# A second, root-scaled copy of the FFN input with its high and low halves side by side, and 512-column products from up piece 6 on

## What is computed

```python
h = rms_norm(x, ffn_pre_norm[l])
u = h @ w_up                                   # 1024 -> 5632
u = sum(up[:, t:t + S] * conv_w[t] for t in range(3))   # along the tokens
gate, val = jnp.split(u, 2, axis=-1)
x = x + rms_norm((jax.nn.gelu(gate) * val) @ w_down, ffn_post_norm[l])
```

## Time and profile before

| | us |
|---|---|
| median of 3 runs | 1029.5 (1029.44 to 1029.59) |
| span of the profiled execution | 1027.2 |
| TensorE busy in the span | 1013.0 (99%) |
| VectorE busy | 680.7 (66%) |
| ScalarE busy | 587.5 (57%) |
| GpSimd busy | 130.7 (13%) |
| moved from HBM | 168.7 MB |

### The profile page before, as it was taken

How to read it: one execution, slowest core, us unless ns; L and a number is a source line. 1 busy time by engine, 2 the same in 40 slices (tenths; PEclk the granted TensorE clock), 3 DMA queues, 4 the chain that set the end, 5 groups by cost and what they waited for, 6 DMA issues and landing times.

```text
span 1027.2 us, 15935 instructions
## 1 busy us (share of the span) xinstructions
PE 1013.0 (99%) x6244; PEld 908.5 (88%) x6244; DVE 680.7 (66%) x932; ACT 587.5 (57%) x859; POOL 130.7 (13%) x257
## 2 busy tenths in 40 slices
PE   8999999999999999999999999999999999999997
PEld 7889999888888999999888899998888889999996
DVE  5635566655596887878865355666555869787877
ACT  5657666565446654555575666565653457455553
POOL 3353124000002000000025221230000020000000
PEclk9999999999999999999999999999999999999999
DMA  8554345444444646555454534464344645545551
GB/s 259 178 177 155 122 141 168 161 165 164 144 150 157 203 169 203 170 200 172 168 190 159 174 124 128 150 205 164 124 144 164 204 145 166 203 169 201 174 195 41
DMA packets 109037, 170.78 MB, mean 166 GB/s; under 512 B 3377, under 2 KB 72804, under 8 KB 108964
## 3 DMA queue, kind: packets, MB, share of 16 engines
q1 hardware_dynamic: 107676, 166.88, 48.8%
q10 hardware_dynamic: 1208, 2.63, 0.7%
q0 software_dynamic: 80, 0.26, 0.1%
HBM read 168.72 MB, written 1.05 MB: 165 GB/s over the span
## 4 chain that ended last, share of the span: by engine, by line
PE 95%; DVE 1%; ACT 1%; DMA 1%; issue 1%; DVEq 0%; SPq 0%; POOL 0%; POOLq 0%
PE bank L1418 28%; PE bank L1420 28%; PE bank L1419 28%; PE bank L1783 2%; PE bank L1684 1%; PE bank L1705 1%; PE bank L1776 1%; PE bank L1693 1%; PE bank L1721 1%; PE bank L1728 1%; PE bank L1773 1%; DMA w_raw<-in_w_in_dram 1%; PE bank L1735 1%; PE bank L1741 1%; DVE x_rows L1233 0%
## 5 line engine op out<-in xcount | busy, mean ns | idle before, releaser
L1053 DVE TENSOR_TENSOR w_lo<-w_raw,w_hi 128x2048 fp32r<-128x2048 f32 (+3 forms) x174 | 364.3, 2094 | 160.6 <-ACT w_hi L700 160.5
L700 ACT ACTIVATE w_hi<-w_raw 128x2048 fp32r<-128x2048 f32 (+3 forms) x174 | 304.7, 1752 | 50.3 <-PE bank L1420 48.8
L1418 PE MATMUL bank<-w_hi,hT_lo 128*128 128x512 f32 (+2 forms) x700 | 258.4, 369 | 1.5 <-DVE hT_lo L1127 0.8
L1420 PE MATMUL bank<-w_hi,hT_hi 128*128 128x512 f32 (+2 forms) x700 | 252.9, 361 | 0.0
L1419 PE MATMUL bank<-w_lo,hT_hi 128*128 128x512 f32 (+2 forms) x700 | 252.5, 361 | 0.0
L1418 PE MATMUL bank<-hT_hi,w_lo 128*128 128x256 f32 x704 | 199.4, 283 | 0.7 <-DVE hT_lo L1080 0.7
L1420 PE MATMUL bank<-hT_hi,w_hi 128*128 128x256 f32 x704 | 199.2, 283 | 0.0
L1419 PE MATMUL bank<-hT_lo,w_hi 128*128 128x256 f32 x704 | 199.2, 283 | 0.0
L1418 PEld LDWEIGHTS bank<-w_hi,hT_lo 128*128 128x128 f32 x700 | 131.5, 188 | 17.8 <-issue 3.0
L1420 PEld LDWEIGHTS bank<-w_hi,hT_hi 128*128 128x128 f32 x700 | 131.4, 188 | 14.1
L1419 PEld LDWEIGHTS bank<-w_lo,hT_hi 128*128 128x128 f32 x700 | 131.6, 188 | 13.0
(11 more groups left out here) (215 smaller groups left out, 1250.1 us busy)
## 6 DMA issues: line engine op xcount, KB each, us to landing
w_raw<-in_w_up_dram SPq DMA_DIRECT2D x44, 1024.0 KB, 4.9
w_raw<-in_w_in_dram SPq DMA_DIRECT2D x36, 1024.0 KB, 4.9
w_raw<-in_w_in_dram SPq DMA_DIRECT2D x36, 768.0 KB, 4.2
w_raw<-in_w_down_dram SPq DMA_DIRECT2D x22, 1024.0 KB, 4.8
w_raw<-in_w_out_dram SPq DMA_DIRECT2D x8, 1024.0 KB, 4.9
w_raw<-in_w_in_dram SPq DMA_DIRECT2D x8, 672.0 KB, 4.0
w_raw<-in_w_branch_mla_dram SPq DMA_DIRECT2D x4, 1024.0 KB, 4.9
w_raw<-in_w_branch_diff_dram SPq DMA_DIRECT2D x4, 1024.0 KB, 4.8
```

The lines of the kernel that those rows point to most:

```text
L700: nc.scalar.activation(w_hi[:, n % RING, 0:nk * cols], raw[:, n % RING, 0:nk * cols], ACT.Copy).then_inc(hi_done, 1)
L1053: V.tensor_tensor(w_lo[:, n % RING, s], raw[:, n % RING, s], w_hi[:, n % RING, s].bitcast(F32), ALU.subtract).then_inc(lo_done, 1)
L1418: PE.matmul(dst, lhs[1], rhs_hi, start=start, stop=False)
L1420: return PE.matmul(dst, lhs[0], rhs_hi, start=False, stop=stop)
```

## The change

A second copy of the input, `scaled_input`, is made in the middle of the first up pieces: it holds for each block k the high part and, beside it, the low part of the input times `token_scale`, as one row of 512 columns. It is made in four steps: GpSimd adds `hT_hi` and `hT_lo` into `merged` (128x2048), GpSimd multiplies it by `token_scale` once up piece 0 is scaled, ScalarE rounds it into the high half in its step of up piece 3, GpSimd subtracts to get the low half. Up pieces 0 to 5 stay as they were. From piece 6 on (`SCALED = 6`) a pair of (half, k) takes two products: `w_lo` with the high half (256 columns), and `w_hi` with high and low side by side (512 columns). The halves of the bank hold two partial sums, one bank for each half of the channels, so that a piece takes two banks and waits for piece c - 2. VectorE no longer multiplies: it adds the two partial sums with a `tensor_reduce` over an innermost axis of two, straight from PSUM.

```diff
+                whole = merged[:].rearrange("p t (k q) -> p (t k) q", q=SEQ)
+                pool.wait_ge(turn_emptied, l * NTURN + (TURN_BEFORE["ffn"] + len(FFN_LO)))
+                nc.gpsimd.tensor_tensor(whole, hT_hi[:].bitcast(F32), hT_lo[:].bitcast(F32), ALU.add)
+                pool.wait_ge(up_scaled_done, l * 2 * NU + 1)
+                pool.drain()
+                nc.gpsimd.tensor_tensor(whole, whole, token_scale...broadcast_to([P, KD, SEQ]), ALU.mult).then_inc(scaled_whole, 1)
+                pool.wait_ge(scaled_hi, l + 1)
+                pool.drain()
+                nc.gpsimd.tensor_tensor(scaled[:, :, 1, :], whole, scaled[:, :, 0, :].bitcast(F32), ALU.subtract).then_inc(scaled_lo, 1)
...
+                            if c == 3:
+                                act.wait_ge(scaled_whole, l + 1)
+                                nc.scalar.activation(scaled[:, :, 0, :], merged..., ACT.Copy).then_inc(scaled_hi, 1)
...
-                else:
+                elif c < SCALED:
                     last = V.tensor_tensor(up_scaled[:, c % 2, :, :], bank[4 + c % 4][:]..., token_scale..., ALU.mult)
+                else:
+                    last = V.tensor_reduce(up_scaled[:, c % 2, :, :], up_banks(c).rearrange("p j (s q) -> p j q s", s=2), AX.X, ALU.add)
...
+            def passes_beside(dst, w_parts, k):
+                if k == 0:
+                    PE.matmul(dst, w_parts[0], scaled[:, k, :, :], start=True, stop=False)
+                last = PE.matmul(dst[:, 0:SEQ], w_parts[1], scaled[:, k, 0, :], start=False, stop=False)
+                if k:
+                    last = PE.matmul(dst, w_parts[0], scaled[:, k, :, :], start=False, stop=k == KD - 1)
+                return last
...
+                    if c == SCALED:
+                        pe.wait_ge(scaled_lo, l + 1)
+                        pe.wait_ge(up_scaled_done, l * 2 * NU + (c - 2))
+                    if c > SCALED:
+                        pe.wait_ge(up_scaled_done, l * 2 * NU + (c - 1))
```

More of the change, by code:

```diff
@@ L283, in pieces_2pi @@
     return out + [float(np.float32(rest))]
+SCALED = 6
 def lambda_init(layer):
@@ L370, in build_trunk @@
             up_scaled = sb("up_scaled", [P, 2, 2, SEQ], scope=four)
+            scaled = sb("scaled_input", [P, KD, 2, SEQ], F32R, scope=four)
         with ExitStack() as six:
@@ L373, in build_trunk @@
             par_rows = sb("par_rows", [44, 4 * DEPTH, P], scope=six)
-        bank = [ctx.enter_context(nc.psum_tensor(f"bank{i}", [P, 512], F32)) for i in range(8)]
+        bank = [ctx.enter_context(nc.psum_tensor(f"bank{i}", [P, 512], F32)) for i in range(4)]
+        high_banks = ctx.enter_context(nc.psum_tensor("high_banks", [P, 4, 512], F32))
+        bank += [high_banks[:, i, :] for i in range(4)]
         S_BANK, O_BANK = (bank[4], bank[5]), bank[7]
@@ L415, in build_trunk @@
         root_rows_ready, scales_full, up_scaled_done = sem("root_rows_ready"), sem("scales_full"), sem("up_scaled_done")
+        scaled_whole, scaled_hi, scaled_lo = sem("scaled_whole"), sem("scaled_hi"), sem("scaled_lo")
         lat_squares, lat_normed = sem("lat_squares"), sem("lat_normed")
@@ L506, in build_trunk, with up_banks @@
         root_rows = xn[:, 0, 0:NT * P].rearrange("p (t q) -> p t q", t=NT)
+        def up_banks(c):
+            pair = (c + 1) % 2
+            return high_banks[:, 2 * pair:2 * pair + 2, :]
         token_scale = xn[:, 0, 512:512 + SEQ]
@@ L667, in _ @@
                     root(l, ("pre", t), ffn_squares, l * 2 * NT + (2 * t + 2), 2 * t)
+                whole = merged[:].rearrange("p t (k q) -> p (t k) q", q=SEQ)
[3 more added lines that the diff above has]
+                pool.drain()
+                nc.gpsimd.tensor_tensor(whole, whole, token_scale.rearrange("p (o q) -> p o q", o=1).broadcast_to([P, KD, SEQ]),
+                                        ALU.mult).then_inc(scaled_whole, 1)
+                pool.wait_ge(scaled_hi, l + 1)
+                pool.drain()
+                nc.gpsimd.tensor_tensor(scaled[:, :, 1, :], whole, scaled[:, :, 0, :].bitcast(F32), ALU.subtract).then_inc(scaled_lo, 1)
                 for t in range(NT):
@@ L943, in _ @@
                             u, b = c // 2, c % 2
+                            if c == 3:
+                                act.wait_ge(scaled_whole, l + 1)
+                                nc.scalar.activation(scaled[:, :, 0, :], merged[:].rearrange("p t (k q) -> p (t k) q", q=SEQ), ACT.Copy).then_inc(scaled_hi, 1)
                             act.wait_ge(up_scaled_done, l * 2 * NU + (c + 1))
@@ L1495, in use_piece @@
                     u, b = c // 2, c % 2
-                    if c >= 4:
+                    if 4 <= c < SCALED:
                         pe.wait_ge(up_scaled_done, l * 2 * NU + (c - 3))
+                    if c == SCALED:
[3 more added lines that the diff above has]
+                        pe.wait_ge(up_scaled_done, l * 2 * NU + (c - 1))
                     order = [(k, j) for k in range(8) for j in range(2)] if c == 0 else [(k, j) for j in range(2) for k in range(8)]
@@ L1505, in use_piece @@
                             turn_roots(l)
-                        last = passes(up_half(c, j), (hi[:, k, j * P:(j + 1) * P], lo[:, k, j * P:(j + 1) * P]),
-                                      hT_hi[:, k, :], hT_lo[:, k, :], k == 0, k == 7)
+                        w_parts = (hi[:, k, j * P:(j + 1) * P], lo[:, k, j * P:(j + 1) * P])
+                        if c < SCALED:
+                            last = passes(up_half(c, j), w_parts, hT_hi[:, k, :], hT_lo[:, k, :], k == 0, k == 7)
+                        else:
+                            last = passes_beside(up_banks(c)[:, j, :], w_parts, k)
                     last.then_inc(piece_used, 1)
```

## The result

The changed kernel takes **1045.9 us** (median of four runs, 1044.8 to 1046.5) against 1029.5: a ratio of 1.0158, with a 95% interval of 1.0144 to 1.0173. The forecast was 1042.0, from 1024 to 1052. The profiled execution has a span of 1044.4 us, 17.2 more than before's 1027.2. It is the longest of the four: the spans of the other three are 1042.9, 1042.9 and 1043.0, some 15.7 more than before.

A forecast was written before the change was run, and what follows sets the result against it. TensorE, busy 99% of the span and 95% of the chain, was taken as the bound. Products -6.8, layer's end +2.0 and GpSimd's holds on VectorE +17.3 gave +12.5 us: 1042.0 us against 1029.5, range 1024 to 1052.

The forecast's parts named there:

- The rival without a hold: Long GpSimd instructions don't hold VectorE, so no wait ahead of pieces 2 to 5: -4.8 us, 1024.7 us; chance 0.19.
- the walk: Layer 0's first up pieces followed in time: GpSimd's 4.6 us instructions hold VectorE, TensorE idles; +17.3 us for both layers.
- that order: GpSimd's add starts before the split for piece 2 and holds it: 9.3 us a layer.
- the first idle time: TensorE ahead of piece 2, waiting for the split held by GpSimd's add: 1.5 us, or 0 if the split goes first.
- The second: TensorE idle ahead of piece 3, behind GpSimd's multiplication: 4.8 us, 5.1 in the other order.
- the third: TensorE idle ahead of piece 5, whose split stands behind GpSimd's subtraction: 3.0 us.
- The clock: TensorE falls to 1.2 GHz behind idle times: 0 to 10 us more, up to 1052, inside the forecast's case (0.63).
- the two orders: GpSimd's add or the split for piece 2 first: 9.3 or 8.1 us a layer, 16.2 to 18.6 for both; 17.3 taken.
- TensorE's gain: Up pieces 6 to 21: a pair of products costs 346.8 ns instead of 360.0, 512 pairs, -6.8 us.
- The sum out of PSUM: VectorE's reduce of 1024 elements takes 1.22 us, 0.53 more than the scaling now, its jump between terms free.
- the steady order: From piece 6 on, VectorE's room of 1.7 us shrinks to 0.4, so the longer sum stays hidden.
- the layer's end: Longer sums make down pieces 9 and 10 late: 1.0 us a layer, +2.0 us in all, between 0 and 3.

The follow-up runs named there:

- the preparation alone: Kernel before plus GpSimd's three bulk instructions, the buffer and ScalarE's copy, old products kept, copy unused: 1050.4 us, ratio 1.0199.
- the last two pieces plain: Changed kernel with up pieces 20 and 21 on the old three products of 256 columns and the old scaling: 1043.5 us, ratio 1.0133.
- the copy moved: Changed kernel with the scaled copy 64 floats further on in SBUF: 1044.5 us, measured once.
- eighths: Changed kernel with each of GpSimd's three bulk instructions cut into eight of 256 elements: 1036.4 us, ratio 1.0065.

## Why the prediction was right, and where it was off

**The mechanism held.** The prediction said that the two engines take turns by whole instructions, also where one of them lasts 4.6 us. It lasts 4.55 to 4.64 (forecast 4.6 to 4.7). The rival without a hold said 1024.7; the kernel in which GpSimd only writes shows 1027.3, and with GpSimd reading the preparation alone costs 20.9 us. The Trainium skill's rule that the two of such a pair exclude each other for the whole instruction (SBUF — State Buffer, Who interferes with whom) is borne out by this case's trace, for 4.6 us at a time. The diagonal, which reads one tile and a scalar a partition, has 4.57 us like the others; the walk had not counted it among them.

**The walk, instant by instant.** The split for piece 3 was to end at 352.0 and ended at 351.98; the subtraction was to start at 359.6 and started at 359.22; the split for piece 5 was to end at 366.5 and ended at 366.60. (The stage begins 0.16 us later than in the trace before.) The last agreement is in part luck: the subtraction began 0.4 us early, and between it and the split stood the product of gate and value, with 0.56 us still to work, which the walk had left out. The sum of the first stage was to be 9.3 us in that order, and layer 0 lost 9.23. The shares were different. I named the split as the first held instruction; it was the one ahead of it, the diagonal, because it too is released by the last root. That put the first idle time ahead of the root products and made it 2.4 us (2.55 from start to start, less 0.12) instead of 1.5. The second was 3.5 instead of 4.8, the third 1.7 instead of 3.0. That is 7.6 us; another 1.4 is the clock, which the sum had at nothing (next paragraph). The parts moved and the sum stayed, because VectorE's chain, not TensorE's, sets the end of the stage.

**The clock was in the range (0 to 10 us) and not in the sum.** It did fall. From the trace after, the stretch behind the second idle time:

```profile
352.00:359.00 7.00, 6.96 (x47) 6.96 (x48) 6.41 (x10) 6.92 (x7) 0.00 (x0) 0.79 0.54 177
```

TensorE has no idle time in it, yet the products first start 0.21 us apart, 1.2 GHz, then 0.12, and the piece takes 7.15 us instead of 5.76. In layer 0 those 1.4 us lie inside the next wait for VectorE, which is why that one is shorter than forecast. In layer 1 the same happens behind the first idle time, also inside a later one; but behind the last, ahead of piece 5 (2.96 us), nothing follows that could hide it, and piece 5 takes 7.35 us (879.44 to 886.79): 1.6 us on the path. VectorE's chain is 0.3 later as well (its split for piece 5 ends at 879.38, where 512.5 behind layer 0's would be 879.10). 9.23 + 1.6 + 0.3 is the 11.0 of layer 1 to within 0.15. In the profiled execution the stage cost 20.2 us where I took 17.3: 1.6 is the clock, 0.3 the later chain, and the remaining 1.0 that I had taken a value between the two orders (16.2 to 18.6) where both layers ran in the dearer one.

The 1.6 belongs to that execution. In the two kernels with the same first stage (the last two pieces plain, the copy moved) the clock stayed up behind layer 1's first idle time and fell behind the second, ahead of piece 3, which takes 8.5 and 8.4 us. So TensorE reached piece 5 late by itself, with 0.3 us of idle time or less ahead of it, and piece 5 took 5.86: the slow stretch lay inside the wait for VectorE, and the layer's stage took 50.08 us. The spans of the changed kernel's other three executions fit that. By these two traces the stage costs 18.8 us, 1.5 over the 17.3, close to the dearer order's 18.6 and with nothing of the clock on the path.

**TensorE's gain was too large by a quarter.** The prices of the earlier trace rows are those of the down products (512 columns of `g_hi`) and of the old up products (256 of `hT_hi`). The new rows, start to start, have:

```profile
412.05 0.40 PE L1457 MATMUL high_banks<-scaled_input,w_hi 128*128 128x512 f32 x1
412.29 0.28 PE L1455 MATMUL high_banks<-scaled_input,w_lo 128*128 128x256 f32 x1
412.41 0.40 PE L1457 MATMUL high_banks<-scaled_input,w_hi 128*128 128x512 f32 x1
```

0.36 us in these rows for a pair; over whole pieces 0.3494, where I had 0.3468. The medians are 233 ns from a wide start to the next narrow one (forecast 226.8) and 117 from narrow to wide (120.0). A piece falls from 5.753 to 5.590 us, 0.163 instead of 0.21, and 32 of them give 5.2 us instead of 6.8. (The other 0.4 of the -5.6 is in the 14 down pieces between them, 5.45 us instead of 5.47.) The step that was off is that both prices come from runs of equal products and that I set them side by side. Why a pair costs 3 ns more stays open. The alternation isn't shown to be the cause: where two wide products of the copy follow each other (k = 0 of the second half) they start 232 ns apart, not 227. The shift by 64 elements didn't change it.

**The sum out of PSUM** takes 1.221 us, forecast 1.22, with the jump for free. In the steady order it is hidden, as forecast. At the layer's end the walk gave 1.0 a layer and it is 1.2: two waits ahead of the first products of down 9 and 10,

```profile
511.61 0.47 PE L1447 MATMUL bank<-w_hi,g_lo 128*128 128x512 f32 x1 [0.45 <-DVE g_lo L1147]
517.68 0.47 PE L1447 MATMUL bank<-w_hi,g_lo 128*128 128x512 f32 x1 [0.39 <-DVE g_lo L1147]
```

in about equal parts instead of 0.7 and 0.3. The kernel with plain last pieces has neither.

**The whole.** Forecast -6.8 + 2.0 + 17.3 = 12.5; in the profiled execution -5.6 + 2.4 + 20.2 = 17.0, where the -5.6 holds everything from up 6 to down 8. All three terms erred to the same side: 1.2, 0.4 and 2.9 us, and of the last 1.6 is the clock, which I had kept for the range. For the other three, with the stage as in the two traces just named, it is -5.6 + 2.4 + 18.8 = 15.6. The median, 16.4 over before, is the time of two of these: 15.7 in the span and 0.7 outside it (3.0 us between time and span, 2.3 in the forecast), which no term of mine has and no run explains.

## What to carry to other kernels

A bulk instruction on GpSimd that reads SBUF isn't free because GpSimd is: it holds VectorE's splits, outer taps and products of gate and value, which read SBUF, for its whole length (4.6 us here), while VectorE's scaling out of PSUM passes (0.69 us). So its price is read from VectorE's idle time in that window, and its release belongs on the event behind which VectorE goes idle (the end of its last split), not on the arrival of its data; one such choice was worth 24 us here. If no window is as long as the instruction, cut it (eighths took half of the loss away), or let VectorE do it in half the time. And where a forecast leaves TensorE idle for some us in one piece, give the last such gap of a stage a clock term as a range, here 0 to 1.6 us a layer: what the clock takes behind the earlier ones hid inside the next wait, and behind the last it came in one execution and not in others of the same stage.

## What the runs showed that I had not expected

- Beside GpSimd's writes (a memset, nothing read) the row of VectorE's diagonal grew from 0.29 to 1.80 us, though the split behind it started and ran as ever (2.29). The row ends with the first write in both layers; what keeps it open no run shows.
- TensorE's clock fell to 1.2 GHz behind three of the six idle times: that of 3.6 us in layer 0, where the first product (352.04) was already slow, and in layer 1 those ahead of the root products (2.55 us) and ahead of piece 5 (3.08), where TensorE ran at 2.4 GHz for 1.4 to 1.5 us more (to 853.37 and 880.79) before it slowed. The slow stretches were 2.9 to 3.4 us long. The equal idle time ahead of the root products of layer 0 (2.55 us) had no such thing behind it. In the two other kernels with this stage the clock fell in each layer behind the idle time ahead of piece 3 (3.3 to 3.7 us) and nowhere else in the stage, for 3.1 us once and for 5.9 to 6.1 three times.
- The products of the copy: 233 ns behind a wide one and 117 behind a narrow one, against the 226.8 and 120.0 of the earlier trace rows.
- Between the device time and the span lie 1.7 to 2.5 us in most executions, but 2.7 to 3.5 in two of the changed kernel's four and in some of the writes-only kernel and of the eighths. What makes the difference isn't known.
